# Experts' stage with exact high and low gather and scatter, a scatter in two parts and 2 MB weight units

## Chip, cores and metric

The kernel runs on one core of one Trainium2 chip. The metric is the device time of one execution in microseconds (us), the median of several runs; lower is better.

## What is computed

One step of a one-layer decoder, for 256 prompt tokens and 64 sample tokens (320 in all) that share the weights. A mixer (GLA attention and causal pooling) comes first, then a layer norm, then a mixture of experts, then a second layer norm. The change lies in the experts' stage. Cut to that:

```python
def _moe(x2, w_router, b_router, w_gu, b_gu, w_down, b_down):     # x2: 320 x 1024
    logits = x2 @ w_router + b_router
    top_v, top_i = lax.top_k(logits, 4)                  # 4 of 32 experts for each token
    gate_w = jax.nn.softmax(top_v, axis=-1)
    ...
    def expert_block(xblk, e):                           # the tokens that chose expert e
        hh = xblk @ w_gu[e] + b_gu[e]                    # 1024 x 2048 weights
        gate = jnp.minimum(hh[:, :1024], 7.0)
        up = jnp.clip(hh[:, 1024:], -7.0, 7.0)
        act = (up + 1.0) * (gate * jax.nn.sigmoid(1.702 * gate))
        return act @ w_down[e] + b_down[e]               # 1024 x 1024 weights
    ...
    y = y.at[token].add(gate_w * res)
x <- LayerNorm(alpha * h + moe(h))
```

All is float32. The weights of the 32 experts are 12 MB each (1 MB is 1024 x 1024 bytes here), 384 MB together, and each is read once.

## The kernel before

Every engine has its own program, and they meet at semaphores. The mixer ends with products of kind `out`; layer norm, router and ranks of each token tile run between the last of them (`turn_h`, `router`, `ranks`). The 320 tokens are tiles of 128, 128 and 64 rows (`TILES`), and each expert takes at most 64 tokens (`CAP`). More tokens for an expert would be worked off in an extra loop at the end.

The experts are worked off in 16 pairs, each pair by `pair_of_blocks` on TensorE (PE), ScalarE (ACT) and VectorE (DVE). For a pair of experts e and e+1, PE does in this order: `turn_up(e)` (8 transposes of the up product), `scatter` of the pair before, `expert_up` of e+1, `turn_slots`, `gather` for the next pair, `expert_down` of e, `turn_up(e+1)`, `expert_up` of e+2, `expert_down` of e+1. A gather is a product of the token rows `hrow` with a one-hot matrix of slots; its result is copied by ACT to `xgt`. A scatter is a product of the transposed one-hot matrix, which carries the gate weights, with the experts' output `res`; it gives six pieces of 128 (or 64) x 512, and DVE adds each to `y` (`add_pieces`). The pieces go through three PSUM banks, so the fourth has to wait for the first addition. PE runs a float32 product as two instructions, a product on a `float32r` view (`arena_r`, `ring_r`) as one.

The weights come as units of 1 MB, issued by the sync engine (SP) in the fixed order of `UNIT_SEQ`: 8 units for an up product, 4 for a down product. They lie in 16 slots (`SLOTS`). Twelve of the slots serve the mixer first and come free as its products end, so the first 16 units are loaded before the stage begins. After that SP issues unit n when PE has used unit n - 16:

```python
was_up, e, j = unit_at(n - SLOTS)
...
sp.wait_ge(up_used if was_up else down_used, count)
```

GpSimd (POOL) issues the small loads: `b_down` and the gains and biases of the second layer norm (`ln2`), both after the last router product. Between the first up product and the first pair, PE multiplies the gate weights with `b_down` (the line of `bdn_rows`), and DVE starts `y` with the six results. The parts named `first_gather`, `route` and `first_onehot` make the first gather, tile by tile, while the last tile is still in the layer norm.

## Time and profile before

| | |
|---|---|
| median of 3 runs | 1321.51 us (1321.49 to 1321.51) |
| the profiled execution | 1328.91 us, its span 1327.0 us |
| PE busy in the span | 1269.0 us (96%) |
| DVE, ACT busy | 437.7 us (33%), 230.6 us (17%) |
| first expert product starts, last ends | 347.74 us, 1302.65 us |
| last weight unit lands | 1289.4 us |
| moved by DMA | 454.19 MB, mean 342 GB/s over the span (417 GB/s in the stage) |
| granted TensorE clock | mean 0.983 |

The span runs from the first to the last instruction of the program; times inside it are counted from its start. MB and GB/s of the profile are in units of 10^6 and 10^9 bytes.

### The profile page before, as it was taken

The page shows a single profiled execution, that of the slowest core. Times are in us where ns is not written, and L with a number is a line of the kernel's source. Part 1 is how long each engine was busy: PE and PEld are TensorE (multiplying, and loading weights), DVE is VectorE, ACT ScalarE, POOL GpSimd, SP SyncE. Part 2 cuts the span into 40 slices and gives each one's busy share as a digit, 9 for nine tenths or more (in the row PEclk, how much of TensorE's full clock was granted, in tenths as well). Part 3 has the DMA queues.
Part 4 walks back from the last instruction along what each step waited for, and adds up shares of the span by engine and source line. Part 5 has one row for each costly group of instructions (what it writes and reads, how often), then busy time and mean ns, then how long its engine had stood idle before and what let it go on. Part 6 is the DMA issues. An engine that isn't in the chain of part 4 may idle for free.

```text
span 1327.0 us, 16958 instructions
## 1 busy us (share of the span) xinstructions
PE 1269.0 (96%) x6497; PEld 702.9 (53%) x6497; DVE 437.7 (33%) x871; ACT 230.6 (17%) x360; POOL 29.3 (2%) x43
## 2 busy tenths in 40 slices
PE   6999999999899999999999999999999999999993
PEld 6999999987543434343443434343443434343431
DVE  4665565654322241313132231313132231313135
ACT  4633334410101011011101011011101011011112
POOL 0000010200000000000000000000000000000002
PEclk9999999999789999999999999999999999999997
DMA  9524444673589999999999999999999999999981
GB/s 379 193 106 143 162 155 157 262 292 127 198 332 377 418 416 417 417 418 417 417 417 416 416 418 418 417 418 417 417 417 416 417 416 418 417 418 417 417 337 41
DMA packets 81366, 454.19 MB, mean 342 GB/s; under 512 B 7437, under 2 KB 7565, under 8 KB 44456
## 3 DMA queue, kind: packets, MB, share of 16 engines
q1 hardware_dynamic: 77264, 439.63, 82.0%
q0 software_dynamic: 4064, 14.03, 3.1%
q8 instruction: 27, 0.44, 0.1%
q14 instruction: 11, 0.09, 0.0%
HBM read 447.44 MB, written 6.31 MB: 342 GB/s over the span
## 4 chain that ended last, share of the span: by engine, by line
PE 92%; DVE 4%; issue 2%; DMA 1%; ACT 0%; DVEq 0%; SPq 0%; ACTq 0%
PE bank L919 33%; PE bank L942 17%; PE bank L649 13%; PE bank L898 10%; PE bank L963 4%; PE bank L717 3%; PE bank L692 2%; PE bank L928 1%; PE bank L931 1%; PE bank L774 1%; PE bank L857 1%; DVE arena L1610 1%; DVE arena L1597 1%; PE bank L906 1%; PE bank L741 1%
## 5 line engine op out<-in xcount | busy, mean ns | idle before, releaser
L919 PE MATMUL bank<-ring,arena 128*64 128x512 f32 x1536 | 349.6, 595 | 0.0
L919 PEld LDWEIGHTS bank<-ring,arena 128*64 128x64 f32 x1536 | 119.5, 137 | 205.8 <-issue 205.8
L649 PE MATMUL bank<-arena_r,ring_r 128*128 128x320 f32 x848 | 182.8, 316 | 0.0
L942 PE MATMUL bank<-ring,arena 128*64 128x512 f32 x768 | 169.3, 593 | 1.3 <-ACT arena L1212 1.3
L1588 DVE TENSOR_TENSOR arena<-bank,arena 128x512 f32<-128x512 f32 x64 | 41.2, 686 | 359.5 <-PE bank L931 359.5
L649 PEld LDWEIGHTS bank<-arena_r,ring_r 128*128 128x128 f32 x848 | 138.7, 188 | 1.9 <-issue 1.8
L1581 DVE COPY arena<-bank 128x512 f32<-128x512 f32 x32 | 22.1, 692 | 327.8 <-PE bank L919 327.6
L898 PE MATMUL bank<-arena 128*128 128x128 f32 x720 | 127.9, 308 | 0.0
L919 PE MATMUL bank<-arena 128*64 128x512 f32 x512 | 119.4, 593 | 1.4 <-ACT arena L1194 1.4
L963 PE MATMUL bank<-arena 128*128 128x512 f32 (+1 forms) x192 | 93.0, 613 | 21.7 <-DVE arena L1610 15.9
L898 PEld LDWEIGHTS bank<-arena 128*128 128x128 f32 x720 | 97.9, 188 | 28.1
L942 PEld LDWEIGHTS bank<-ring,arena 128*64 128x64 f32 x768 | 54.4, 137 | 107.7 <-issue 104.7
L1202 ACT ACTIVATE arena<-bank 128x512 f32<-128x512 f32 x32 | 19.1, 597 | 478.1 <-PE bank L919 478.1
L1274 DVE TENSOR_TENSOR ring_r<-ring,ring_r 128x1024 fp32r<-128x1024 f32 x56 | 67.7, 1222 | 57.4 <-ACT ring_r L1050 57.2
L649 PE MATMUL bank<-ring_r 128*128 128x320 f32 x280 | 85.9, 307 | 0.0
L919 PEld LDWEIGHTS bank<-arena 128*64 128x64 f32 x512 | 41.0, 136 | 70.9 <-issue 70.9
L1212 ACT ACTIVATE arena<-bank 64x512 f32<-64x512 f32 x64 | 37.8, 591 | 195.5 <-PE bank L942 195.1
L963 PEld LDWEIGHTS bank<-arena 128*128 128x128 f32 (+1 forms) x192 | 29.2, 171 | 75.8 <-DVE arena L1610 40.4
L1610 DVE TENSOR_TENSOR arena<-arena,bank 128x512 f32<-128x512 f32 (+1 forms) x96 | 62.9, 681 | 18.8 <-PE bank L963 18.4
L1050 ACT ACTIVATE ring_r<-ring 128x1024 fp32r<-128x1024 f32 x56 | 58.1, 1052 | 20.6 <-PE bank L649 19.3
L942 PE MATMUL bank<-arena 128*64 128x512 f32 x256 | 56.7, 595 | 0.0
L649 PEld LDWEIGHTS bank<-ring_r 128*128 128x128 f32 x280 | 52.7, 188 | 0.2
(213 smaller groups left out, 897.4 us busy)
## 6 DMA issues: line engine op xcount, KB each, us to landing
ring<-in_w_gu SPq DMA_DIRECT2D x192, 1024.0 KB, 14.9
ring<-in_w_down SPq DMA_DIRECT2D x96, 1024.0 KB, 17.8
arena<-in_w_gu SPq DMA_DIRECT2D x64, 1024.0 KB, 13.1
ring<-in_w_mix SPq DMA_DIRECT2D x32, 1024.0 KB, 5.1
arena<-in_w_down SPq DMA_DIRECT2D x32, 1024.0 KB, 16.5
arena<-in_state_gla POOLq DMA_DIRECT2D x4, 1024.0 KB, 10.3
out<-arena POOLq DMA_DIRECT2D x4, 1024.0 KB, 5.4
x_alone<-in_x_t SPq DMA_DIRECT2D x2, 640.0 KB, 4.6
```

The lines of the kernel that those rows point to most:

```text
L649: last = mm(o[:, 0:NT], w[a][:, c, f0:f0 + 128], rhs[b][:, c, :], start=c == 0 and a + b == 0, stop=c == chunks - 1 and a == 1)
L692: last = mm(o[:, 0:256], acts[c][:, t0:t0 + 128], w[:, c, :], start=c == 0, stop=c == KC - 1)
L717: last = mm(o[:, 0:256], xt[a][:, c, t0:t0 + 128], w[b][:, c, :], start=c == 0 and a + b == 0, stop=c == KC - 1 and a == 1)
L898: last = mm(ex[6 + c // 4][:, (c % 4) * 128:(c % 4 + 1) * 128], hrow[0:n, t, c * 128:(c + 1) * 128], onehot[0:n, t, :], start=t == 0, stop ...
L919: last = mm(ex[i][side * CAP:(side + 1) * CAP, :], xgt[:, j, half * CAP:(half + 1) * CAP], w[:, i * D + side * 512:i * D + (side + 1) * 51 ...
L942: last = mm(ex[4][side * CAP:(side + 1) * CAP, :], actt[:, 2 * j + c, :], w[:, c, side * 512:(side + 1) * 512], start=j == 0 and c == 0, s ...
L963: mm(ex[5 + i % 3][0:n, :], slot_t[:, t0:t0 + n], res[:, half * 512:(half + 1) * 512], start=True, stop=True).then_inc(pieces, 1)
L1050: A(half_of(hi, half), half_of(raw, half), ACT.Copy).then_inc(high_ready, 1)
L1212: last = A(res[half * CAP:(half + 1) * CAP, side * 512:(side + 1) * 512], ex[4][side * CAP:(side + 1) * CAP, :], ACT.Copy)
L1274: V.tensor_tensor(half_of(lo, half), half_of(raw, half), half_of(hi, half), ALU.subtract)\
L1588: V.tensor_tensor(dst.rearrange("p (h c) s -> p h c s", h=2), ex[2 + i][:, :].rearrange("p (c h s) -> p h c s", h=2, s=CAP), bias.broadcas ...
L1610: V.tensor_tensor(part, part, ex[5 + i % 3][0:n, :], ALU.add).then_inc(added, 1)
```

## The change

It has five parts.

1. **Gather.** `hrow` is split into a high part (a copy to `float32r`) and a low part (the remainder) by `split_h` on DVE. A gather multiplies both with the one-hot matrix: twice the products, on `float32r` views. It reports each half of the result, ACT copies each half by itself, and the up product waits for the second half only before its third unit. In the pair it stands behind the down product of e.
2. **Scatter.** The gate weight is no longer in the one-hot matrix. It is brought to the slots by six small products in `turn_slots` and applied when ACT copies the output (`keep_output`, high part) and when DVE makes the low part (`low_output`, new). The six pieces take two `float32r` products each, three pieces between the second and third unit of the up product and three behind its last (`between`). `turn_slots` stands between the two units of the down product.
3. **Down bias.** Three copies of gate weights and `b_down` are stacked on 96 partitions as high and low parts, and one `float32r` product gives each result.
4. **Units of 2 MB.** Eight slots of 2 MB; an up product has 4 units, a down product 2. The host lays the weights out so that a unit is one block with 16 KB on each partition.
5. **Places.** `y` takes the place of `hrow`, and the `ln2` values lie where a weight slot is, so POOL loads them once the first unit of the last expert has been used.

```diff
-SLOTS = MORE_AT + MORE
+SLOTS = (MORE_AT + MORE) // 2
+WIDE = 2 * UNIT
-UP_UNITS, DOWN_UNITS = KC, KC // 2
+UP_UNITS, DOWN_UNITS = KC // 2, KC // 4
...
+        LN2_FREE = (NE - 1) * UP_UNITS + 1
...
-                if is_up:
-                    src = w_gu[0, ds(e, 1), j * 128:(j + 1) * 128, :].rearrange("e p n -> p (e n)")
-                    sp.dma_start(dst, src).then_inc(filled[s], 16)
-                else:
-                    src = w_down[0, ds(e, 1), j * 256:(j + 1) * 256, :].rearrange("e (c p) n -> p (e c) n", p=128)
-                    sp.dma_start(dst.rearrange("p (c n) -> p c n", c=2), src).then_inc(filled[s], 16)
+                src = (w_gu if is_up else w_down)[ds(e, 1), j, :, :].rearrange("e p n -> p (e n)")
+                sp.dma_start(dst, src).then_inc(filled[s], 16)
...
-            pool.dma_start(bdn_rows, b_down[0, :, :]).then_inc(bdn_in, 16)
+            for i in range(3):
+                pool.dma_start(bdn_rows[i * NE:(i + 1) * NE, :], b_down[0, :, :]).then_inc(bdn_in, 16)
+            pool.wait_ge(up_used, LN2_FREE)
             pool.dma_start(ln2[0], ln2_g[0:1, :].broadcast_to([128, D])).then_inc(ln2_in, 16)
...
                 for c in range(KC):
                     for t, (t0, n) in enumerate(TILES):
-                        last = mm(ex[6 + c // 4][:, (c % 4) * 128:(c % 4 + 1) * 128], hrow[0:n, t, c * 128:(c + 1) * 128],
-                                  onehot[0:n, t, :], start=t == 0, stop=t == 2)
-                last.then_inc(gathered, 1)
+                        for a in range(2):
+                            last = mm(ex[6 + c // 4][:, (c % 4) * 128:(c % 4 + 1) * 128],
+                                      h_parts[a][t][0:n, c * 128:(c + 1) * 128], onehot[0:n, t, :],
+                                      start=t == 0 and a == 0, stop=t == 2 and a == 1)
+                    if c % 4 == 3:
+                        last.then_inc(gathered, 1)
...
                 for t, (t0, n) in enumerate(TILES):
-                    last = nc.tensor.transpose(ex[5][:, t0:t0 + n], onehot_w[0:n, t, :], ident[0:n, 0:n])
+                    mm(ex[5][:, t0:t0 + n], onehot[0:n, t, :], ident_r[0:n, 0:n], start=True, stop=True)
+                for t, (t0, n) in enumerate(TILES):
+                    for a in range(2):
+                        last = mm(ex[5][:, NT:NT + NE], onehot[0:n, t, :], gw_parts[a][0:n, t, :],
+                                  start=t == 0 and a == 0, stop=t == 2 and a == 1)
                 last.then_inc(slots_turned, 1)
...
+                    if gathers is not None and j % 2 == 0:
+                        pe.wait_ge(xgt_ready, 2 * gathers - 1 + j // 2)
                     pos, landing = where(j)
                     pe.wait_ge(*landing)
...
                     last.then_inc(up_used, 1)
+                    if j % 2 and between:
+                        between[j // 2]()
...
                     if i >= 3:
                         pe.wait_ge(added, pair * 6 + i - 2)
-                    mm(ex[5 + i % 3][0:n, :], slot_t[:, t0:t0 + n], res[:, half * 512:(half + 1) * 512],
-                       start=True, stop=True).then_inc(pieces, 1)
+                    for a in range(2):
+                        last = mm(ex[5 + i % 3][:, :], slot_t[:, t0:t0 + 128], res_parts[a][:, half * 512:(half + 1) * 512],
+                                  start=a == 0, stop=a == 1)
+                    last.then_inc(pieces, 1)
...
                 turn_up(e)
-                if not first:
-                    scatter(pair - 1, e)
-                expert_up(units(True, 2 * p + 1, m), 1)
-                turn_slots(pair + 1)
+                expert_up(units(True, 2 * p + 1, m), 1,
+                          between=() if first else [lambda: scatter(pair - 1, e, 0), lambda: scatter(pair - 1, e, 1)])
...
-                else:
+                if not first:
+                    pe.wait_ge(added, pair * 6 - 2)
+                expert_down(e, units(False, 2 * p, m), between=turn_slots)
+                if not last:
                     if not first:
                         pe.wait_ge(added, pair * 6)
                     gather(pair + 2)
-                expert_down(e, units(False, 2 * p, m))
...
+            def low_output(idx, half):
+
+                dve.wait_ge(res_high, idx + 1)
+                p0 = half * CAP
+                for side in range(2):
+                    f0 = side * 512
+                    last = V.scalar_tensor_tensor(res_parts[1][p0:p0 + CAP, f0:f0 + 512], ex[4][side * CAP:(side + 1) * CAP, :],
+                                                  slot_w[p0:p0 + CAP, 0:1], res_parts[0][p0:p0 + CAP, f0:f0 + 512],
+                                                  ALU.mult, ALU.subtract)
+                last.then_inc(res_ready, 1)
```

How PE's instructions move shows best where no loop registers stand between them. In the first pair, behind the transposes of expert 0, PE's rows before are the up product (L919) of expert 1, the slots' transposes (L906), the gather (L898), the down product (L942), the transposes for expert 1 (L928, L931), the next up product and the second down product:

```order
L919 MATMUL bank<-ring,arena 64x512 x32
L906 MATMUL bank<-arena 128x128 x2
L906 MATMUL bank<-arena 128x64
L898 MATMUL bank<-arena 128x128 x24
L942 MATMUL bank<-arena 64x512 x16
L928 MATMUL bank<-arena 128x128 x4
L931 MATMUL bank<-arena 128x128 x4
L919 MATMUL bank<-ring,arena 64x512 x32
L942 MATMUL bank<-ring,arena 64x512 x16
```

In the changed program the same place reads as follows (L948 is now the up product, L974 the down product, L928 and L931 the turning of slots and of gate weights, L919 the gather, L960 and L963 the transposes):

```order
L948 MATMUL bank<-ring,arena 64x512 x32
L974 MATMUL bank<-arena 64x512 x8
L928 MATMUL bank<-arena_r 128x128 x2
L928 MATMUL bank<-arena_r 128x64
L931 MATMUL bank<-arena_r 128x32 x6
L974 MATMUL bank<-arena 64x512 x8
L919 MATMUL bank<-arena_r 128x128 x48
L960 MATMUL bank<-arena 128x128 x4
L963 MATMUL bank<-arena 128x128 x4
L948 MATMUL bank<-ring,arena 64x512 x32
L974 MATMUL bank<-ring,arena 64x512 x16
```

The gather has twice the products and now stands behind the down product; the turning of the slots stands inside it.

The scatter is seen in the last pair. Before, PE's rows there are the transposes, the scatter (L963), and then the whole up product:

```order
L928 MATMUL bank<-arena 128x128 x4
L931 MATMUL bank<-arena 128x128 x4
L963 MATMUL bank<-arena 128x512 x4
L963 MATMUL bank<-arena 64x512 x2
L919 MATMUL bank<-arena 64x512 x16
L919 MATMUL bank<-ring,arena 64x512 x16
```

In the changed program L998 is the scatter:

```order
L960 MATMUL bank<-arena 128x128 x4
L963 MATMUL bank<-arena 128x128 x4
L948 MATMUL bank<-arena 64x512 x16
L998 MATMUL bank<-arena_r 128x512 x6
L948 MATMUL bank<-ring,arena 64x512 x16
L998 MATMUL bank<-arena_r 128x512 x6
```

It is cut in two, and an up product's half stands ahead of each part. On DVE, also in the last pair, the additions of the pieces stood before in one row of six ahead of the copy of the up product:

```order
L1610 TENSOR_TENSOR arena<-arena,bank 128x512 x4
L1610 TENSOR_TENSOR arena<-arena,bank 64x512 x2
L1575 TENSOR_SCALAR arena<-arena 128x64 x2
L1575 TENSOR_SCALAR arena<-arena 64x64
L1575 TENSOR_SCALAR arena<-arena 128x64 x2
L1575 TENSOR_SCALAR arena<-arena 64x64
L1581 COPY arena<-bank 128x512
```

Now three of them stand ahead of that copy (L1633) and three behind it:

```order
L1662 TENSOR_TENSOR arena<-arena,bank 128x512 x3
L1633 COPY arena<-bank 128x512
L1662 TENSOR_TENSOR arena<-arena,bank 128x512
L1662 TENSOR_TENSOR arena<-arena,bank 64x512 x2
```

The one-hot matrices with weights (L1575) are gone from DVE.

## Rows read from the trace of the kernel before

**Rows 1.** Page: GB/s moved by DMA in 40 equal slices of the span

```profile
GB/s 379 193 106 143 162 155 157 262 292 127 198 332 377 418 416 417 417 418 417 417 417 416 416 418 418 417 418 417 417 417 416 417 416 418 417 418 417 417 337 41
```

**Rows 2.** Waits of PE, 377 to 1286 us: who for whom, total, times, longest

```profile
PE bank L963 <- DVE arena L1610: 15.9, 15, 1.1
PE bank L963 <- ACT arena L1212: 4.6, 15, 0.4
```

**Rows 3.** Timeline of PE, one pair and more: start, us, instruction, idle before

```profile
605.97 0.66 PE L928 MATMUL bank<-arena 128*128 128x128 f32 x4
...
613.72 14.27 PE L919 MATMUL bank<-ring,arena 128*64 128x512 f32 x63
627.92 0.64 PE L906 MATMUL bank<-arena 128*128 128x128 f32 x3
628.49 8.52 PE L898 MATMUL bank<-arena 128*128 128x128 f32 x48
...
643.96 0.66 PE L928 MATMUL bank<-arena 128*128 128x128 f32 x4
...
644.99 13.95 PE L919 MATMUL bank<-ring,arena 128*64 128x512 f32 x64
...
687.69 0.64 PE L906 MATMUL bank<-arena 128*128 128x128 f32 x3
```

**Rows 4.** DMA, two windows of 60 us (600:660, 1160:1220): issues, KB, median us to landing

```profile
ring<-in_w_gu SPq DMA_DIRECT2D x12, 1024.0 KB, 13.3
...
ring<-in_w_gu SPq DMA_DIRECT2D x16, 1024.0 KB, 17.8
```

**Rows 5.** Four single issues (1236.6, 1249.8, 1251.5, 1270.9 us): landing min/median/max

```profile
DMA to landing us min/median/max: 14.8/14.8/14.8
...
DMA to landing us min/median/max: 19.1/19.1/19.1
...
DMA to landing us min/median/max: 19.9/19.9/19.9
...
DMA to landing us min/median/max: 18.5/18.5/18.5
```

**Rows 6.** Windows: us, PE, PEld, DVE, ACT, POOL busy, PEclk, DMA share, GB/s

```profile
349.70:1289.40 939.70, 917.32 (x4231) 385.96 (x4229) 226.13 (x506) 98.52 (x171) 0.00 (x0) 0.99 1.00 411
```

**Rows 7.** Timeline of SP, its first issue in the stage, and that issue's landing

```profile
349.71 5.52 SPq L515 DMA_DIRECT2D arena<-in_w_down  x4
...
DMA to landing us min/median/max: 4.9/4.9/4.9
```

**Rows 8.** Line L717: durations in ns (min/median/max), first and last start

```profile
L717 PE MATMUL bank<-ring_r,arena_r x192: 277/280/283, 46.6 to 80.2; 128*128 128x256 f32 x192
```

**Rows 9.** Timeline around the stage's start

```profile
322.91 9.85 PE L857 MATMUL bank<-arena 64*128 64x128 f32 x32 [0.56 <-issue]
343.06 3.31 PE L857 MATMUL bank<-arena 128*128 128x128 f32 x16 [0.34 <-DVE arena L1521]
347.74 7.09 PE L919 MATMUL bank<-arena 128*64 128x512 f32 x32 [1.38 <-ACT arena L1194]
361.63 0.55 PE L1001 MATMUL bank<-arena 128*32 128x128 f32 x3
363.12 7.72 PE L1009 MATMUL bank<-arena 32*128 32x512 f32 x12 [0.94 <-DVEq L1675]
371.61 1.11 PE L928 MATMUL bank<-arena 128*128 128x128 f32 x4 [0.77 <-DVE arena L1681]
```

**Rows 10.** Windows of lost clock, columns as in rows 6

```profile
325.30:345.70 20.40, 17.55 (x70) 14.41 (x69) 6.17 (x32) 2.99 (x6) 1.59 (x3) 0.50 0.25 83
366.30:376.40 10.10, 9.33 (x22) 3.30 (x22) 5.12 (x10) 0.63 (x1) 0.00 (x0) 0.50 0.58 240
```

**Rows 11.** Chain that ended last, the stage's end: start, us, what

```profile
1295.54 7.11 PE bank L942 x32
```

**Rows 12.** Page, costliest groups: x count, busy us, mean ns, idle before

```profile
L1581 DVE COPY arena<-bank 128x512 f32<-128x512 f32 x32 | 22.1, 692 | 327.8 <-PE bank L919 327.6
```

More of the change, by code:

```diff
@@ L156 @@
 ARENA = MISC + 64
-H = 0
-Y = 3072
-XGT = 6144
-OHW = 7168
-ACTT = 7552
-G1 = 8064
-OH = 8704
-U1 = 9088
-SG = 9600
-HG = 10112
-HU = 10624
-RES = 11136
-RK = 12352
-GW = 12832
-MSK = 12928
-LG = 13024
-MX = 13120
-RT = 13152
-LISTS = 13536
-GWT = 14120
-BDR = 14440
-LN2 = BDR + D
-ST = LN2 + 2 * D
+Y = 0
+RK = 3072
+GW = 3552
+MSK = 3648
+LG = 3744
+RES = 3840
+MX = 4864
+RT = 4872
+LISTS = 5256
+XGT = 5816
+ACTT = 6840
+SLOT_T = 7352
+WS = 7672
+G1 = 7680
+U1 = 8192
+LOW1 = 8704
+SG = 9728
+HIGH_H = VR
+LOW2 = KLT
+OH = 14336
+IDR = 14720
+HG = 14848
+HU = 15360
+BDR = 15872
+GWT = 16896
+GWR = 17216
+LOW0 = 17408
 MORE_SLOTS = 18432
+LN2 = MORE_SLOTS
 def build(nc, x_p, x_s, state_gla, state_pool, w_gk2, w_grp,
@@ L311, in build @@
         low = ar[0:1, LISTS + 4 * NID + RANKS:LISTS + 4 * NID + 2 * RANKS]
-        filled = [sem(f"slot{i}_filled") for i in range(SLOTS)]
+        filled = [sem(f"slot{i}_filled") for i in range(MORE_AT + MORE)]
         bank_full = [sem(f"bank{i}_full") for i in range(8)]
@@ L850, in released, with first_gather @@
                 pe.wait_ge(bank_free[n], LAST_USE[n])
-            def first_gather(tiles, first):
-                for c in range(KC):
+            def first_gather(tiles, half, first):
+                for c in range(4 * half, 4 * half + 4):
                     for t in tiles:
                         n = TILES[t][1]
-                        last = mm(ex[6 + c // 4][:, (c % 4) * 128:(c % 4 + 1) * 128], hrow[0:n, t, c * 128:(c + 1) * 128],
-                                  onehot[0:n, t, :], start=first and t == tiles[0] and c % 4 == 0, stop=not first,
-                                  skip_group_check=True)
+                        for a in range(2):
+                            last = mm(ex[6 + half][:, (c % 4) * 128:(c % 4 + 1) * 128], h_parts[a][t][0:n, c * 128:(c + 1) * 128],
+                                      onehot[0:n, t, :], start=first and t == tiles[0] and a == 0 and c % 4 == 0,
+                                      stop=not first and a == 1, skip_group_check=True)
                 return last
@@ L880, in _ @@
             pe.wait_ge(onehot_early, 1)
-            first_gather(ORDER[:2], True)
+            pe.wait_ge(parts_ready, 2)
+            for half in range(2):
+                first_gather(ORDER[:2], half, True)
             turn_h(1, 5)
@@ L981, in pair_of_blocks @@
                     gather(pair + 2)
[L982 to L983 removed]
                     turn_up(e + 1)
[L985 to L987 removed]
+                    expert_up(units(True, 2 * p + 2, m), 0, gathers=pair + 2)
                 pe.wait_ge(res_ready, e + 1)
@@ L992, in _ @@
             pe.wait_ge(onehot_ready, 1)
-            first_gather(ORDER[2:], False).then_inc(gathered, 1)
+            pe.wait_ge(parts_ready, 3)
+            for half in range(2):
+                first_gather(ORDER[2:], half, False).then_inc(gathered, 1)
             released(0)
             released(1)
-            pe.wait_ge(xgt_ready, 1)
-            expert_up(units(True, 0), 0)
+            expert_up(units(True, 0), 0, gathers=1)
             pe.wait_ge(soft4_done, 1)
@@ L1602, in gated, with add_pieces @@
                 V.tensor_tensor(actt[:, :, :], u1[:, :, :], sg[:, :, :], ALU.mult).then_inc(act_ready, 1)
-            def add_pieces(pair):
-                for i in range(6):
+            def add_pieces(pair, part):
+                for i in range(3 * part, 3 * part + 3):
                     t, half = i // 2, i % 2
```

239 lines of the change are left out of this document (144 added, 95 removed).

## The prediction

> **What bounds the kernel now.** I read the page's slices first. From slice 14 on DMA moves 416 to 418 GB/s without a break [rows 1], so the stage looks bound by the weight loads. The waits say otherwise: between 377 and 1286 us PE waits 20.5 us in all, only inside the scatter (L963), for an addition or for ACT, and never for a weight [rows 2]. The timeline of PE gives its period: the slots' transposes (L906) stand at 627.92 and at 687.69 us, so a pair takes PE 59.77 us [rows 3]. A pair reads 24 units, 25.17 million bytes, which at 417 GB/s is 60.35 us [rows 1]. So the loads are the slower of the two by 0.6 us a pair. PE does not feel it, because 16 MB lay in the slots when the stage began. The stock shrinks: the median time from issue to landing grows from 13.3 us (window from 600 us) to 17.8 us (from 1160 us) [rows 4], while one issued onto idle queues lands after 4.9 us [rows 7]. PE has its last product at 1302.65 us [rows 11], 13.3 us behind the last landing at 1270.9 + 18.5 = 1289.4 us [rows 5]. The kernel is bound by PE, with the loads close behind: time taken from PE comes back only until the loads bind. So I need two end times, that of PE and that of the loads.
>
> **PE's pair.** Each term is a difference of starts in [rows 3] or a count times a row.
> - Scatter: from the first transposes of a pair (605.97) to its up product (613.72) are 7.75 us, where the same transposes elsewhere take 644.99 - 643.96 = 1.03. The scatter costs 6.7 us, its waits included. It becomes 12 float32r products of 512 columns. The row of such products is L717 with 256 columns: 288 of them (3 tiles x 4 units x 24) between 46.6 and 80.3 us, 117 ns each [rows 8]. Twice the columns give 0.22 us; the upper bound is the present float32 instruction's 0.43 us for 512 columns (an up product's 64 run two side by side, 32 x 0.43 = 13.95 us [rows 3]). I take 0.22, the nearer kind: 2.6 us (at most 5.2).
> - Gather: 8.5 us for 48 instructions (L898) now. Then again 48, of 128 columns each, as float32r. If they cost no more than the 256-column ones they take 48 x 0.117 = 5.6 us; if the weight loads of 64 rows cost as now, up to 8.5. I take 6.0, near the row of their kind.
> - Turning the slots: 627.92 to 628.49, 0.57 us now; then 9 float32r products at 0.117 or more, 1.2 us.
> - New wait: the down product waits for the fourth addition of a pair. DVE copies the up product (0.69 us [rows 12]) between the third and fourth addition, so the fourth ends near 1.5 us after the up product, PE's second scatter part near 1.3. I take 0.3 us. Behind that wait are the down product and SP's release of its slots. The two waits of rows 2 go: half an up product, 6.9 us, lies between the parts.
> - DVE and ACT: `low_output` adds 2 x 0.69 us a block, the two rows of one-hot matrices with weights go. DVE sits idle 328 us before L1581 alone [rows 12], which hides it; without that cover it would cost 2.8 us a pair.
>
> Sum: 59.77 - 6.7 + 2.6 - 8.5 + 6.0 - 0.57 + 1.2 + 0.3 = 54.1 us a pair, 5.7 less (bounds 53.3 and 59.2).
>
> **The stage's start.** The first gather (tiles 2 and 0) takes 9.85 us, the second 3.31, and then up to 347.74 ACT copies both halves [rows 9]. With the first as 32 instructions of half the columns' time I take 2.3 us off (from 0 to 6). The second can hand over its first half after half its length, so its copy and the other half overlap: 1.7 us off. The stage then starts at 347.7 - 4.0 = 343.7 us (338 to 348). The new splits of `h` on DVE, two passes for each tile, about 2.5 us a tile by row 12's rate, lie where DVE waits for PE's products or for the router. The bias: from 361.63 to the first transposes at 371.61 are 10 us [rows 9], with 12 instructions in 7.72 us. Six float32r products make DVE's six additions the bound, 6 x 0.72 = 4.3 us, plus a second DVE pass: 3.5 us less, so the gap is 6.5.
>
> **PE's end.** 1302.65 - 4.0 - 3.5 - 14 x 5.7 - 5 (what the first and the last pair save) = 1210 us.
>
> **The loads' end.** Here 2 MB units matter. Landings: 8 KB rows (`w_gu`), 7 units from 1236.6 + 14.8 to 1249.8 + 19.1, 2.50 us each; 4 KB rows (`w_down`), 7 units from 1251.5 + 19.9 to 1289.4, 2.56 us each [rows 5]. Each of 16 DMA engines moves 8 rows of 8 KB in 2.50 (0.3125 us a row) or 16 of 4 KB in 2.56 (0.160). Another 4 KB costs 0.1525, so a row has 0.0075 of its own. A 16 KB row is 0.3125 + 2 x 0.1525 = 0.6175: 8 of them make a 2 MB unit in 4.94 us. Were the row's own cost nothing, 4.88; if longer rows gain nothing, 5.00; at today's mean (60.35 / 12) 5.03. I take 4.92, between the line and its lower end, as the first figure hangs on landings read to 0.1 us.
>
> By the Trainium skill, "DMA: Bandwidth & Descriptors", section "Where 436 GB/s comes from", the ceiling is 435 GB/s at SBUF's ports, by which a 2 MB unit would take at least 4.82 us, an estimate from that page; by it the loads would end 18 us sooner than in my sum. The same page of the skill puts an HBM limit of about 358 GB/s for a core beside it; this trace disagrees, with 417 GB/s over 900 us.
>
> Eight units, 16 MB as now, are in place before the stage. The ninth is issued when PE has used the first: its 16 instructions take 3.43 us (64 in 13.7). To its first byte go 4.9 - 2.5 = 2.4 us. So the loads start at 343.7 + 5.8 = 349.5. Up(0) frees four units, 19.7 us of loads, done at 369; the next slot comes free after up(0), the bias, the transposes and 3.4 us: 343.7 + 13.7 + 6.5 + 1.1 + 3.4 = 368.4, with 2.4 us latency 370.8, more at half clock, which the old trace had from 366.3 to 376.4 [rows 10]. I take 4 us of idle queues. Before, this idle and more of its kind was 939.7 us [rows 6] less 368 units x 2.515 = 14 us. Then 184 units: 184 x 4.92 = 905.3. The `ln2` loads, 1 MB in 4 KB rows, now fall into the loaded stretch: 2.6. The loads end at 349.5 + 4 + 905.3 + 2.6 = 1261.4 us, 51 us behind what PE could do. **So PE will wait for weights, and the loads set the end.** The moved `b_down` copies fall where the queues are idle (198 GB/s in slice 11 [rows 1]) and cost nothing; in the loaded stretch they would cost 1 us.
>
> **The end.** The last unit is worked off in 3.43 + 0.6 = 4.0 us. From the last product to the end are 1327.0 - 1302.65 = 24.35 us; `low_output` adds 1.4, six additions that wait no more for float32 products take off about 1.2: 24.6. Span: 1261.4 + 4.0 + 24.6 = 1290.0, 37.0 less than 1327.0. The profiled execution took 1328.91 us, 7.4 more than the median; I take the difference off the median: 1321.5 - 37.0 = **1284.5 us**.
>
> **Rivals.**
> 1. The loads bind but gain nothing from long rows (5.03 instead of 4.92): 184 x 0.11 = 20 us more, 1305 us. For it: a mean rate constant for 900 us looks like a ceiling. Against it: 8 KB rows land faster than 4 KB rows.
> 2. The clock. The granted clock was 0.50, its level of 1.2 GHz, from 325.3 to 345.7, after the gather's short products of 64 rows, and from 366.3 to 376.4, in the bias products of 32 rows [rows 9, 10]; each time PE had instructions nearly all the time. The new gather streams half as long per weight load as the old, and PE then waits for weights. If each gather costs the clock for the shorter of those stretches, 10.1 us, PE loses 5 us a pair and ends at 1210 + 14 x 5.05 = 1281 us, behind the loads: 1281 + 24.6 - 1327 = -21.4, 1300 us.
> 3. The same for the longer stretch, 20.4 us, 10.2 lost a pair: PE's end 1210 + 143 = 1353, span 1377.5, **1372 us, slower**. It decides from 6.6 us lost a pair (14 x 6.6 = 92, PE's old end). Against both: the old gather, 8.5 us with 64-row products too, kept full clock in all 14 pairs (clock 0.99 over the stage [rows 6]), and up products follow at once. The Trainium skill, "TensorE: Matmul & The Clock Gate", section "HAM oscillation", tells of a kernel that lost the clock again and again as it waited for weights; the trace of before has no such wait to show.
> 4. PE gains but the loads were the true bound already, so nothing moves: 1321 us. Rows 2 and 11 speak against it.
>
> **Numbers.** Forecast case 0.64, rival 1 0.16, rival 2 0.11, rival 3 0.06, rival 4 0.03. The forecast's bounds: 4.88 takes off 7 us and a start at 338 another 6, so 1270; rival 1 reaches 1305 at the top, which also holds rival 2. The range 1270 to 1306 leaves out rivals 3 and 4 and some of the tails. Less than 0.2% (2.6 us) cannot be told from no change: faster 0.91, same 0.03, slower 0.06.
>
> **What would show it.** A pair takes about 54 us while the stock of 16 MB lasts (PE gains one 2 MB unit a pair), then 12 x 4.92 = 59 us, with PE waiting for weight loads about 5 us a pair; about 426 GB/s; the last landing near 1261 us and PE's last product 4 us behind it; gather near 6 us, scatter parts 1.3 us each without idle. I am wrong if a pair stays near 60 us with no wait for a load (PE slower than I think), if GB/s stays at 417 (rival 1), or if the clock row shows less than full in the stage (rivals 2, 3).

## The result and the profile after

The changed kernel takes **1340.0 us** (median of 4 executions, 1338.3 to 1341.0), and the ratio to the kernel before is 1.0112, with an interval of 1.0083 to 1.0141: slower by 1.1%, where 1284.5 us was forecast. (Executions of the kernel before take 1321.0 to 1331.8 us, most of them near 1321.5 or 1329, with a mean clock from 0.990 down to 0.980; every ratio is to executions of it on the same chip.) In the profiled executions the span went from 1327.0 to 1337.8 us.

The page after, its slices (PEclk is the granted TensorE clock in tenths; the last row answers to [rows 1]):

```profile
span 1337.8 us, 16365 instructions
...
PE   6999999999899999999999999999999999999993
...
PEclk9999999998788998989898898989898998989897
...
GB/s 378 196 109 131 172 142 158 281 267 126 212 370 329 427 420 404 430 398 429 422 429 402 428 401 410 417 421 430 402 427 400 428 422 417 414 399 429 402 269 41
```

DMA now swings between 400 and 430 GB/s, so the loads are no longer back to back. PE is busy without a break, by the profile, which models the ends of its products, and the clock row dips all through the stage. Of the waits of PE over the whole span (who for whom, total, times, longest, answering to [rows 2]) none is for a weight. These are the three longest; the two for DVE, which makes the low part of the output in L1670, are single waits of the last pair:

```profile
PE bank L681 <- ACT ring_r L1088: 10.2, 1, 10.2
PE bank L974 <- DVE arena_r L1670: 3.1, 1, 3.1
PE bank L998 <- DVE arena_r L1670: 3.1, 1, 3.1
```

So PE sets the end. Its timeline over one pair (start, us, instruction) answers to [rows 3]. L919 is the gather, L960 and L963 are transposes, L948 up products, L974 down products, L998 the scatter's two parts, L928 and L931 `turn_slots`:

```profile
637.05 9.38 PE L919 MATMUL bank<-arena_r 128*128 128x128 f32 x48
646.35 1.11 PE L960 MATMUL bank<-arena 128*128 128x128 f32 x4
647.26 1.06 PE L963 MATMUL bank<-arena 128*128 128x128 f32 x4
648.25 14.45 PE L948 MATMUL bank<-ring,arena 128*64 128x512 f32 x64
662.53 7.03 PE L974 MATMUL bank<-ring,arena 128*64 128x512 f32 x32
669.50 0.66 PE L960 MATMUL bank<-arena 128*128 128x128 f32 x4
...
670.52 7.09 PE L948 MATMUL bank<-arena 128*64 128x512 f32 x32
677.54 1.66 PE L998 MATMUL bank<-arena_r 128*128 128x512 f32 x6
679.13 7.09 PE L948 MATMUL bank<-ring,arena 128*64 128x512 f32 x32
686.15 1.67 PE L998 MATMUL bank<-arena_r 128*128 128x512 f32 x6
687.75 3.65 PE L974 MATMUL bank<-ring,arena 128*64 128x512 f32 x16
691.33 0.66 PE L928 MATMUL bank<-arena_r 128*128 128x128 f32 x3
691.92 0.94 PE L931 MATMUL bank<-arena_r 128*128 128x32 f32 x6
692.79 3.65 PE L974 MATMUL bank<-ring,arena 128*64 128x512 f32 x16
696.38 10.30 PE L919 MATMUL bank<-arena_r 128*128 128x128 f32 x48
```

Three things are to be seen. The scatter comes near the forecast: two parts of 1.60 us (677.54 to 679.13, and 686.15 to 687.75) where 1.3 each were forecast, without a wait. The gather does not: 9.38 and 10.30 us where 6.0 was forecast and 8.52 stood before. And the same four transposes take 1.11 us behind the gather and 0.66 us later on: the clock is at half there. Two windows put on such stretches, and one behind them (columns as in [rows 6]):

```profile
581.00:591.20 10.20, 10.20 (x36) 6.70 (x38) 3.27 (x6) 1.23 (x2) 0.00 (x0) 0.50 1.01 430
642.50:649.30 6.80, 6.80 (x26) 5.26 (x28) 0.83 (x2) 0.60 (x1) 0.00 (x0) 0.50 1.00 426
651.00:663.00 12.00, 12.00 (x60) 3.91 (x58) 1.09 (x3) 0.25 (x1) 0.00 (x0) 1.00 1.00 411
```

A clock of 0.50 is the 1.2 GHz level, 1.00 is 2.4 GHz. PE was busy for all of the 10.2 and 6.8 us in which it had lost half of its clock. In each of the 15 gathers of the stage's pairs the clock falls, 3.2 to 5.7 us after the gather's start: 4 times for 6.8 us, 10 times for 10.2 us, and the first for 13.7 us. Fourteen pairs go by from the first of these gathers (393.47) to the last (1241.37), 60.56 us each, against 59.77 before.

### The profile page after: what moved, and what is told of

Its sections match the earlier page's. It is cut to its first block, busy times and chain, and to the rows that moved or that the text cites. A ratio compares the mean times of both kernels' runs of the same rounds, so it can differ in the third digit from the quotient of the medians.

```text
span 1337.8 us, 16365 instructions
## 1 busy us (share of the span) xinstructions
PE 1295.3 (97%) x6587; PEld 746.3 (56%) x6587; DVE 467.8 (35%) x812; ACT 245.3 (18%) x394; POOL 30.4 (2%) x45
## 4 chain that ended last, share of the span: by engine, by line
PE 96%; DVE 2%; DMA 1%; ACT 0%; issue 0%; DVEq 0%; SPq 0%; ACTq 0%
PE bank L948 35%; PE bank L974 17%; PE bank L666 13%; PE bank L919 11%; PE bank L998 4%; PE bank L734 3%; PE bank L709 2%; PE bank L960 2%; PE bank L963 2%; PE bank L791 1%; PE bank L931 1%; PE bank L875 1%; PE bank L928 1%; PE bank L758 1%; DMA ring<-in_w_mix 1%; PE bank L721 1%
## 5 line engine op out<-in xcount | busy, mean ns | idle before, releaser
L948 PE MATMUL bank<-ring,arena 128*64 128x512 f32 x1536 | 360.1, 626 | 0.0
L948 PEld LDWEIGHTS bank<-ring,arena 128*64 128x64 f32 x1536 | 111.2, 145 | 227.3 <-issue 227.3
L974 PE MATMUL bank<-ring,arena 128*64 128x512 f32 x768 | 171.0, 594 | 3.1 <-DVE arena_r L1670 3.1
L919 PE MATMUL bank<-arena_r 128*128 128x128 f32 x720 | 146.7, 343 | 0.0
L919 PEld LDWEIGHTS bank<-arena_r 128*128 128x128 f32 x720 | 124.2, 234 | 31.8 <-issue 12.2
L1633 DVE COPY arena<-bank 128x512 f32<-128x512 f32 x32 | 22.1, 692 | 279.9 <-PE bank L948 279.4
L948 PE MATMUL bank<-arena 128*64 128x512 f32 x512 | 114.9, 602 | 0.0
L1670 DVE SCALAR_TENSOR_TENSOR arena_r<-bank,arena,arena_r 64x512 fp32r<-64x512 f32 x64 | 48.0, 750 | 187.0 <-ACT arena_r L1256 186.6
L974 PEld LDWEIGHTS bank<-ring,arena 128*64 128x64 f32 x768 | 52.8, 137 | 107.7 <-issue 100.9
L1320 DVE TENSOR_TENSOR ring_r<-ring,ring_r 128x1024 fp32r<-128x1024 f32 x56 | 67.7, 1223 | 56.8 <-ACT ring_r L1088 56.6
L948 PEld LDWEIGHTS bank<-arena 128*64 128x64 f32 x512 | 36.0, 139 | 71.3 <-issue 71.1
L1256 ACT ACTIVATE arena_r<-bank,arena 64x512 fp32r<-64x512 f32 x64 | 43.7, 683 | 147.0 <-PE bank L974 146.6
L974 PE MATMUL bank<-arena 128*64 128x512 f32 x256 | 58.4, 598 | 0.0
L998 PE MATMUL bank<-arena_r 128*128 128x512 f32 x192 | 53.3, 413 | 3.1 <-DVE arena_r L1670 3.1
L998 PEld LDWEIGHTS bank<-arena_r 128*128 128x128 f32 x192 | 33.4, 188 | 34.8 <-issue 24.7
```

Of the source, the lines that this page charges most:

```text
L919: last = mm(ex[6 + c // 4][:, (c % 4) * 128:(c % 4 + 1) * 128], h_parts[a][t][0:n, c * 128:(c + 1) * 128], onehot[0:n, t, :], start=t == 0 ...
L948: last = mm(ex[i][side * CAP:(side + 1) * CAP, :], xgt[:, 2 * j + c, half * CAP:(half + 1) * CAP], w[:, c, i * D + side * 512:i * D + (sid ...
L974: last = mm(ex[4][side * CAP:(side + 1) * CAP, :], actt[:, 4 * j + c, :], w[:, c, side * 512:(side + 1) * 512], start=j == 0 and c == 0, s ...
L998: last = mm(ex[5 + i % 3][:, :], slot_t[:, t0:t0 + 128], res_parts[a][:, half * 512:(half + 1) * 512], start=a == 0, stop=a == 1)
L1256: last = A(res_parts[0][p0:p0 + CAP, side * 512:(side + 1) * 512], ex[4][side * CAP:(side + 1) * CAP, :], ACT.Copy, scale=slot_w[p0:p0 + C ...
L1320: V.tensor_tensor(half_of(lo, half), half_of(raw, half), half_of(hi, half), ALU.subtract)\
```

## The experiments

Two theories stood at the start. **A**: the clock. The new gather streams little for each load of weights, the clock falls to half under it, and PE loses some 4 us a pair; with the clock kept, PE is faster than the loads and the time is near the forecast. **B**: not the products but the gather's new place costs the time. Unless it says otherwise, an edit is to the changed kernel.

| run | gather at work, us | pair, us (first / loads bound) | mean clock | median, us | ratio to before, interval |
|---|---|---|---|---|---|
| changed kernel | 9.1 to 10.9 | 60.6 / - | 0.929 | 1340.0 | 1.011 (1.008 to 1.014) |
| e1_float32 | 8.5 | 57.1 / 58.8 | 0.981 | 1299.4 | 0.982 (0.979 to 0.986) |
| e1_filler | 9.6 | 58.2 / - | 0.981 | 1305.5 | 0.991 (0.986 to 0.995) |
| e1_pad | 5.4 | 54.0 / 58.8 | 0.979 | 1300.1 | 0.983 (0.980 to 0.986) |
| e1_quarters | 4 x 1.9 | 56.8 / 58.8 | 0.982 | 1295.5 | 0.980 (0.977 to 0.984) |
| e2_both | 4 x 1.5 | 54.9 / 58.8 | 0.978 | 1298.5 | 0.977 (0.974 to 0.981) |
| e2_rows8 | 4 x 1.5 | 54.9 / 59.8 | 0.983 | 1310.5 | 0.987 (0.984 to 0.990) |
| e2_first | 4 x 1.5 | 54.9 / 58.8 | 0.983 | 1292.7 | 0.973 (0.969 to 0.977) |
| e2_units | 8.5 | 59.8 / - | 0.990 | 1326.8 | 0.999 (0.997 to 1.001) |
| e3_ln2 | 4 x 1.5 | 54.9 / 58.8 | 0.984 | 1288.1 | 0.970 (0.968 to 0.972) |
| e3_grouped | 5.9 to 8.1 | 54.6 / 58.8 | 0.966 | 1297.8 | 0.978 (0.975 to 0.982) |
| e4_thin | 15.4 to 17.2 | 67.0 / - | 0.900 | 1436.6 | 1.082 (1.078 to 1.087) |

The gather is timed from its start to that of the next instruction. A pair is the difference of two gathers' starts; the first value holds while the stock of 16 MB lasts. Gather, pair and mean clock are those of the profiled execution, the median is that of all executions.

### The cause: four ways to keep the clock

**e1_float32** leaves the low part out of the gather and runs the high part as float32, two instructions a product, in the same place:

```diff
-                        for a in range(2):
-                            last = mm(..., h_parts[a][t][0:n, c * 128:(c + 1) * 128], onehot[0:n, t, :],
-                                      start=t == 0 and a == 0, stop=t == 2 and a == 1)
+                        last = mm(..., h_parts[0][t][0:n, c * 128:(c + 1) * 128].bitcast(f32),
+                                  onehot[0:n, t, :].bitcast(f32), start=t == 0, stop=t == 2)
```

> The gather of every pair as float32 products of the high part alone (the low part of h is left out of these gathers), at the place it has in the changed kernel. Theory A (the clock falls in the gather because its float32r products stream too thinly between weight loads): the gather takes 8.5 us as in the kernel before and the clock stays at full speed in the stage; a pair is 57.2 us of PE (56.3 of the changed kernel at full clock, less 7.6, plus 8.5), less than the 58.8 us of the loads, so the loads bind: about 1295 us. Theory B (it is the place: gather and transposes behind each other after the down product): the clock falls in every pair as before, a pair is near 62 us, about 1365 us.

**e1_filler** adds work: one product of 512 columns, whose result nobody reads, behind each of the gather's eight chunks.

```diff
                     if c % 4 == 3:
                         last.then_inc(gathered, 1)
+                    mm(ex[2][:, :], h_parts[0][0][:, 0:128], h_parts[0][0][:, 0:512], start=True, stop=True)
```

> One float32r product of 512 columns, whose result nothing reads, after each of the eight chunks of the gather: 8 x 0.22 = 1.7 us more work for PE in a pair. Theory A: the clock stays at full speed, a pair is 58.1 us, just under the loads: about 1297 us, 43 faster with more work. If the clock is not what the changed kernel lost its time by: 15 x 1.7 = 26 us slower, about 1366 us.

**e1_pad** makes the third tile's 64 rows 128, with zeros in the rows of `h_parts` that hold no token:

```diff
-                                      h_parts[a][t][0:n, c * 128:(c + 1) * 128], onehot[0:n, t, :],
+                                      h_parts[a][t][:, c * 128:(c + 1) * 128], onehot[:, t, :],
```

> The last token tile padded from 64 to 128 rows in the gather (zero rows), so all 48 products are 128 x 128 and PE never changes between tiles of 64 and 128 rows. Same count of products. Theory A: 48 x 0.112 = 5.4 us for the gather, streaming in 48% of the time instead of 33%; the clock stays full, a pair is 54.1 us, the loads bind, about 1293 us, with PE waiting for weights 4 to 5 us a pair. Theory B: the clock still falls in each pair and the time is nearer to 1300 to 1310 us.

**e1_quarters** keeps the products and spreads them: a quarter of the gather inside the down product ahead of it, one behind it, and two inside the first unit of the next up product.

```diff
-                    gather(pair + 2)
+                    gather_quarter(pair + 2, 1)
                     turn_up(e + 1)
-                    expert_up(units(True, 2 * p + 2, m), 0, gathers=pair + 2)
+                    expert_up(units(True, 2 * p + 2, m), 0, gathers=pair + 2, quarters=True)
```

> The same gather products in four quarters, two around the second half of the down product and two between the first chunks of the next up product. No instruction is added or taken away. Theories A and B: no thin stretch is longer than 3 us, the clock stays full, a pair is 56.3 us and the loads bind: about 1295 us. If the clock is not the cause: no change against 1340 us.

All four have medians of 1296 to 1306 us. Theory B falls with the first: same place, a gather of 8.5 us, and 41 us less. The filler is the strictest of them. It gives PE 2.0 us more to do in every pair (9.6 instead of 7.6 us at full clock) and takes away no product, no wait and no change of height, and the median is 34 us lower. It does not keep the clock every time, though: six of its ten executions took 1304.8 to 1305.7 us with a mean clock of 0.981, the other four 1323.0 to 1325.6 us with 0.966 or 0.965. Where those four lost it isn't shown, as none of them was profiled; all ten stay below the changed kernel. In one window, 660 to 1200 us, the changed kernel, then the filler (columns of [rows 6]):

```profile
660.00:1200.00 540.00, 540.00 (x2473) 247.01 (x2471) 140.23 (x243) 64.38 (x117) 0.00 (x0) 0.92 0.99 416
```

```profile
660.00:1200.00 540.00, 540.00 (x2639) 244.63 (x2637) 147.98 (x257) 65.68 (x119) 0.00 (x0) 1.00 1.01 428
```

PE is busy for all 540 us in both; at clock 1.00 it gets through 2639 products instead of 2473, some 74 of them the filler's. The same window of e1_float32, e1_pad and e1_quarters:

```profile
660.00:1200.00 540.00, 535.32 (x2584) 231.67 (x2580) 145.40 (x253) 65.75 (x121) 0.00 (x0) 1.00 1.01 428
...
660.00:1200.00 540.00, 505.53 (x2568) 220.18 (x2562) 142.53 (x248) 67.16 (x123) 0.00 (x0) 1.00 1.01 428
...
660.00:1200.00 540.00, 532.99 (x2591) 230.50 (x2590) 144.67 (x252) 65.38 (x123) 0.00 (x0) 1.00 1.01 428
```

The expected times were 4 us (float32), 7 us (padding) and 8.5 us (filler) too low; that of e1_quarters was right to 1 us. In e1_filler PE is still the bound, at 58.2 us a pair and without a wait for a weight, where I had counted on the loads. In e1_pad the last weight lands at 1262.2 us as reckoned, but the clock falls to half in the last products: the last down product takes 8.78 us, as in e1_filler, and 7.09 in e1_quarters.

**e3_grouped** adds nothing and takes nothing away. It puts the gather's products in another order, so that full and half height alternate less:

```diff
-                for c in range(KC):
-                    for t, (t0, n) in enumerate(TILES):
+                for half in range(2):
+                    for t, (t0, n) in enumerate(TILES):
+                        for c in range(4 * half, 4 * half + 4):
```

> The changed kernel with the gather's products in another order: for each half of the columns first the 16 products of tile 0 and 1, then the 8 of tile 2 (64 rows) in one row, so that the height of the products changes 4 times instead of 16. Theory S (the change of height costs, 50 to 95 ns each): the gather takes 5.6 to 6.2 us at full clock instead of 7.6. Theory H (a product of 64 rows is itself slow): it stays at 7.6. For the clock no cure is expected for sure: the stream gets denser than in the changed kernel and stays thinner than in the padded one. If the clock still falls in each pair: 14 x 1.5 to 2.5 us less than 1340, about 1310 to 1320 us; if it is kept, about 1297 us.

Its timeline, three gathers:

```profile
612.66 6.00 PE L920 MATMUL bank<-arena_r 128*128 128x128 f32 x48
618.60 0.66 PE L961 MATMUL bank<-arena 128*128 128x128 f32 x4
...
668.12 6.00 PE L920 MATMUL bank<-arena_r 128*128 128x128 f32 x48
674.06 0.91 PE L961 MATMUL bank<-arena 128*128 128x128 f32 x4
...
726.94 6.43 PE L920 MATMUL bank<-arena_r 128*128 128x128 f32 x48
733.30 1.11 PE L961 MATMUL bank<-arena 128*128 128x128 f32 x4
```

Theory S of its expectation holds: 6.00 us at full clock, the very term of the prediction. The same 48 products need 7.6 us in the changed kernel's order (four quarters of 1.91 us by their starts in e1_quarters, at full clock). So this order is a cure in part only: in or right behind 6 of the 15 gathers the clock is lost, for 3.4 to 10.2 us (mean over 660 to 1200 us: 0.97). I had put the median at 1310 to 1320 us for "falls in each pair" and 1297 for "kept"; it is 1297.8, since the loads bind and PE has 4 us of room in each pair.

**e4_thin** is the test from the other side. It starts from e1_pad, where all products have 128 rows, and cuts each into two of 64 columns:

```diff
-                    for t, (t0, n) in enumerate(TILES):
+                    for s, t in ((0, 0), (0, 1), (0, 2), (1, 0), (1, 1), (1, 2)):
...
-                                      h_parts[a][t][:, c * 128:(c + 1) * 128], onehot[:, t, :],
+                                      h_parts[a][t][:, c * 128:(c + 1) * 128], onehot[:, t, s * 64:(s + 1) * 64],
```

> The padded kernel, with each product of the gather cut into two of 64 columns: all 96 products have 128 rows, none changes height, and PE is never idle between them; they stream the same columns in all, and load the weights twice as often. Theory A (thin streaming behind full weight loads loses the clock, at any height): if a product of 64 columns takes as long as one of 128 (about 110 ns) the gather takes 10.5 us, the clock falls in every pair, and a pair takes 54.0 + 5 + 4 to 5 = about 63 to 64 us, median about 1380 to 1400 us. Theory H (the change between 64 and 128 rows loses the clock): the clock stays full, a pair takes about 59 us, median about 1300 to 1310 us. If a product of 64 columns takes half as long, the stream is as dense as before the cut and both expect the padded kernel's time.

```profile
654.23 3.65 PE L974 MATMUL bank<-arena 128*64 128x512 f32 x16
...
659.28 3.65 PE L974 MATMUL bank<-arena 128*64 128x512 f32 x16
662.86 16.27 PE L919 MATMUL bank<-arena_r 128*128 128x64 f32 x96
678.95 1.11 PE L960 MATMUL bank<-arena 128*128 128x128 f32 x4
```

Two windows in this gather, before and behind the fall of the clock (columns of [rows 6]):

```profile
662.86:667.60 4.74, 4.74 (x45) 4.74 (x43) 1.49 (x2) 1.37 (x2) 0.00 (x0) 1.00 1.02 432
...
667.80:678.90 11.10, 11.10 (x54) 11.10 (x53) 0.00 (x0) 0.60 (x1) 0.00 (x0) 0.50 1.01 430
```

The clock falls in every gather, for 13.7 or 17.1 us, and the kernel takes 1436.6 us. Theory H, that the change of height loses the clock, falls: there is no such change here. A falls short in size only (1380 to 1400 expected), as the clock was lost for most of the gather itself, 16.1 us instead of 10.5. PE was never idle in it. So a run of products that stream few columns for each load of weights loses the clock by itself.

The run is also twice as long as that of e1_pad, but length alone does not explain the fall: it comes 3.7 to 5.7 us after the gather's start, in 13 of the 15 gathers within 5.36 us, and the padded gather of e1_pad, 5.41 us long, keeps the clock in all 15. Length counts beside it, as e1_quarters shows: the changed kernel's own products keep the clock in pieces of 1.9 us.

### What binds once the clock is kept

**e2_both** joins e1_quarters and e1_pad; **e2_rows8** is the same with each unit fetched in two transfers:

```diff
-                sp.dma_start(dst, src).then_inc(filled[s], 16)
+                for i in range(2):
+                    sp.dma_start(dst[:, i * UNIT:(i + 1) * UNIT], src[:, i * UNIT:(i + 1) * UNIT]).then_inc(filled[s], 16)
```

> The changed kernel with the gather in quarters and its third tile padded to 128 rows, both at once. Theory A (with the clock kept, the weight loads set the end): PE alone would need 54.0 us a pair (measured in the padded version while the stock lasted) against 58.8 us of loads, so the second cure adds nothing to the first: the last weight lands near 1262 us as in the padded version, PE keeps its clock to the end, median near 1292 us. Rival C (PE sets the end): the pair loses another 2.8 us against the quarters alone, 14 x 2.8 = 39 us less than 1295.5, about 1257 us.

> The same kernel as e2_both with each 2 MB unit fetched by two transfers of 1 MB, whose rows are 8 KB again instead of 16 KB; slots, waits and products stay. Theory A: a unit takes 2 x 2.50 = 5.00 us instead of 4.90, so 184 x 0.10 = 18 us more than e2_both, about 1311 us, and 60.0 us a pair while the loads bind. Rival 1 of the prediction (long rows gain nothing): the same time as e2_both, within 2 us.

The second cure on top of the first gives nothing that can be told (ratio 0.977 and 0.980, intervals overlap), although PE's pair is 1.9 us shorter while the stock lasts. Its waits between 1000 and 1200 us say why:

```profile
PE bank L949 <- DMA ring<-in_w_gu: 6.8, 8, 1.2
PE bank L978 <- DMA ring<-in_w_down: 2.2, 3, 0.7
PE bank L949 <- DMA arena<-in_w_gu: 1.4, 2, 1.2
```

PE waits for weights, and the window from 660 to 1200 us shows it idle for 28 us with DMA at 428 GB/s (540.00 - 512.27):

```profile
660.00:1200.00 540.00, 512.27 (x2559) 217.60 (x2556) 141.97 (x248) 65.44 (x122) 0.00 (x0) 1.00 1.01 428
```

Rival C falls. The median of e2_both is 6.5 us above the 1292 expected, though the last weight lands at 1264.4 us, 0.1 behind that of e1_quarters: the clock falls three times near the end, so that the last down product takes 8.78 and the scatter behind it 5.49 us, against 7.09 and 3.44. Rival 1 of the prediction falls too: with rows of 8 KB the same window moves 421 GB/s, a pair takes 59.8 us instead of 58.8, the last weight lands at 1278.8 us, and the median is 12 us higher. (Row length and number of transfers change together here; which of the two costs the time is not shown.) I had expected 18 us, from 2.50 us a MB against 2.45; the landings in e2_rows8 are 2.49 us apart.

**e2_units** is the kernel before with the 2 MB units alone (slots, layout, waits of the diff, nothing else).

> The kernel before with nothing of the change but the 2 MB units: 8 slots of 2 MB, rows of 16 KB, waits for a unit twice as large. Theory A (the kernel before is bound by PE): the loads gain 1.3 us a pair that PE does not ask for, so the median stays at 1321.7 us within 2 us. Rival 4 of the prediction (the loads were the bound already): 184 x 0.12 = 22 us less, about 1300 us.

The ratio is 0.999 (0.997 to 1.001), and a pair takes the 59.8 us of before: the faster loads are of no use as long as PE binds. (Its 1326.8 us stand against 1328.8 us, the median of the kernel before on that chip.) Rival 4 falls.

**e2_first** is e2_both with the third tile padded in `first_gather` too, and **e3_ln2** is e2_first with POOL waiting for the last weight unit before it loads `ln2`:

```diff
             pool.wait_ge(up_used, LN2_FREE)
+            pool.wait_ge(*landed(NE * EXP_UNITS - 1))
```

> The same kernel as e2_both with the third tile padded in the first gather too, so that its first part (8.4 us) has no products of 64 rows. Theory A: that part falls to about 4 to 5.5 us, the clock stays at its full level ahead of the stage or falls for a shorter time, the stage starts 2 to 4 us earlier, and as the loads are released by the first up product, the end moves by as much: about 1289 us. Rival D (the router's chain on DVE, not PE's gather, sets the stage's start): no change against e2_both.

> The same kernel as e2_first, with the two transfers of the last norm's gain and bias released by the landing of the last weight unit instead of by the use of the first up unit of the last block. Theory A (the queue of weight loads sets the end): the three late units that land 5.4, 6.2 and 5.7 us apart come 4.9 us apart again, the last weight lands 2.5 us earlier, PE's longest wait for a weight (2.5 us) goes; if with it the clock stays full in the last products, another 1 to 3 us: 3 to 6 us less than e2_first, about 1288 us. Rival E: the transfers, now last, land after DVE has asked for them, and the end stays where it is or moves back.

The stage's start in e2_both:

```profile
323.06 8.14 PE L875 MATMUL bank<-arena_r 64*128 64x128 f32 x32 [0.56 <-issue]
...
341.44 3.68 PE L875 MATMUL bank<-arena_r 128*128 128x128 f32 x16 [0.34 <-DVE arena_r L1578]
345.04 9.30 PE L949 MATMUL bank<-arena 128*64 128x512 f32 x32
```

And in e2_first:

```profile
322.35 3.76 PE L875 MATMUL bank<-arena_r 128*128 128x128 f32 x32 [0.56 <-issue]
...
333.92 3.67 PE L875 MATMUL bank<-arena_r 128*128 128x128 f32 x16 [0.34 <-DVE arena_r L1578]
337.52 8.80 PE L949 MATMUL bank<-arena 128*64 128x512 f32 x32
```

The first part's 32 instructions take 3.76 instead of 8.14 us, although they work on a third more rows, zeros. In e2_both the clock is at half from 325.7 us on, for 23.9 us, in e2_first from 330.8 on, for 10.2. The stage starts 7.5 us earlier (2 to 4 expected), the last weight lands 8.5 us earlier (1255.9), and the span is 8.6 us shorter (5.8 us in the medians, where the intervals of the ratios overlap). Rival D falls. One of the four executions of e2_first had a mean clock of 0.936 instead of 0.983 and yet took 1295.2 us, 2.5 above the median, which fits that a lost clock costs little while the loads bind. In e3_ln2 the last weights come 4.9 us apart again and the last lands at 1253.3 us, 2.6 us earlier, and PE's longest wait for a weight goes from 2.5 to 1.3 us; the span is 3.4 us shorter, 4.6 us in the medians. So the end did not stay where it was, as rival E has it, by the two traces; the intervals of the ratios overlap here too. The clock in the last products did not come back, though: the last down product takes 8.78 us and the scatter 5.49 in both. This is the lowest median, 1288.1 us, 3.0% below the kernel before (2.8 to 3.2%).

## Why the prediction was wrong

The step that failed is the one on **the clock**, rivals 2 and 3, to which it gave 0.17 together. The reason given against them was that "the old gather, 8.5 us with 64-row products too, kept full clock in all 14 pairs". But the old gather was float32, with two instructions for each product; e1_float32 shows that this kind keeps the clock in the new place too. What the runs show instead is a loss at every one of the 15 new gathers, 4.3 us a pair, which e1_filler, e1_quarters, e3_grouped and e4_thin lay to a long run of thinly streaming products. The prediction had seen that the new gather "streams half as long per weight load as the old" and weighed it too lightly. The nearest row was the first gather of the kernel before, 9.85 us long, 2.4 us into which the clock had fallen, at 325.3 [rows 9, 10]. The clock was lost for 6.8 or 10.2 us a time, near rival 2's 10.1, and rival 2 gave 1300 us, not a loss. What made it rival 3's outcome, a slower kernel, is that further terms were too small, the gather's above all, in which the changes of height stood at nothing:

- **PE's pair**, forecast 54.1 us. Scatter 3.2 instead of 2.6; `turn_slots` 1.46 (691.33 to 692.79) instead of 1.2; the new wait 0 instead of 0.3. That gives 54.1 + 0.6 + 0.3 - 0.3 = 54.7, and e3_grouped, whose gather takes the forecast 6.0, has a pair of 54.6. The gather in the changed order takes 1.6 us more (56.2), and the lost clock the remaining 4.3: 60.56. PE thus loses 6.5 us a pair against the forecast; the prediction had put the point of no gain at 6.6.
- **PE's end**, forecast 1210 us, is 1306.37 + 7.09 = 1313.5. Of the 103 us, 14 x 6.45 = 90 are the pairs' and 1.3 the stage's start (345.0 instead of 343.7); the other 12 lie in the first and the last pair and the up product ahead of them, where the clock was at half too (from 325.0 to 348.9 and from 366.0 to 372.8 us). They are not split further.
- **The stage's start and the bias.** The first gather took 8.4 instead of the 7.6 us implied (9.85 - 2.3). Both stood under a clock at half (from 325.0 us here), so 9.85 us was no price at full clock; e2_units below has that price. The six stacked products and the rest up to the first transposes took 6.7 us (360.8 to 367.6), 6.5 forecast.
- **The loads.** 4.92 us a unit was forecast, 4.90 measured, in every version of 16 KB rows that they bind; 5.00 for 8 KB rows, 4.98 measured. The end of the loads, forecast at 1261.4 us, is 1264.2 in e1_quarters, which makes the same products as the changed kernel at full clock; PE's last product is 4.4 us behind it (4.0 forecast), 24.4 us before the end (24.6), and the span 1293.1 (1290.0). The side of the sum that hangs on "PE will wait for weights" is near the mark once PE keeps its clock, in part because errors offset: 184 units at 4.90 take 3.7 us less than at 4.92, the stage starts 1.3 later, and some 5 us more lie elsewhere and are not split further. (The 417 GB/s "over 900 us" of the prediction hold for some 830 us, 25 slices; over the 940 us of [rows 6] it is 411.) In the changed kernel itself the loads have room, and the last one lands at 1293.6 us because PE frees the slots late.
- **DVE**, costed at nothing, cost nothing in the pairs: PE waits for it in none, and only at the stage's end for `low_output`, twice 3.1 us.
- **The difference of 7.4 us** between the profiled execution and the median was taken off the forecast. The changed kernel has no such second value (1338.3 to 1341.0), so its profiled execution, 1339.7, stands at its median. The profiled execution of e2_units, 1321.65 us, shows where the 7 us lie: its products are those of the kernel before, but its clock is at half from 334.4 us on for 6.8 us, not from 325.2 on for 20.5. The first gather, 9.85 us in [rows 9], takes 6.71 us, and the stage starts at 342.1 instead of 347.7 us:

```profile
322.40 6.71 PE L853 MATMUL bank<-arena 64*128 64x128 f32 x32 [0.56 <-issue]
```

## What to carry to other kernels

A product's price is not its duration in a dense row alone: ask how many columns each load of weights is followed by, and count a long run of short products as a risk for the clock, in the run and behind it, even when the engine never idles. Before halving the streaming time of a run of products, look in the trace for a run of the new kind and read the clock in it and behind it; when it falls, spread the run or pad it (the clock held in all 15 gathers), or order it by height (it held in 9 of 15 gathers). Read the mean clock of several executions too, not of the profiled one alone. And a second bound that is close (here 58.8 us of loads against 59.8 of PE) caps the gain, so that a cure is worth making only up to it.

## What the runs showed of the hardware

- The clock fell to half with PE busy for 100% of the time by the profile, in all 15 gathers of the changed kernel. Waits for weights of up to 1.3 us, again and again, left it at 1.00 from 660 to 1200 us (28 of 540 us in e2_both). Longer single waits went either way: at one of 2.5 us for a weight near the end it fell for 3.4 us in e1_float32, e1_pad, e2_both and e2_first and stayed full in e1_quarters, as it did at one of 2.9 us in e2_rows8. The Trainium skill, "TensorE: Matmul & The Clock Gate", section "HAM oscillation", lays a lost clock to waits for transfers, and section "Why this matters for your kernels" advises against long idle gaps of PE between its bursts. The falls at the waits near the end, in four of the six versions named, point the same way; the loss in the changed kernel is one that no gap explains.
- Going from 128 to 64 rows and back between float32r products of 128 columns costs: 7.6 us for 48 products with 16 changes a gather, 6.0 with 4, so (7.6 - 6.0) / 12 = 0.13 us a change. With the short tile padded, a fifth more rows to work on, the gather took 5.4 us.
- A float32r product of 64 columns takes no less time than one of 128. At full clock the starts in the gather are 112 ns apart in e4_thin (64 columns) and 111 ns in e1_pad (128 columns, all of 128 rows), by the median; at half clock they are 213 ns apart in e4_thin.
- A 2 MB unit in 16 KB rows lands every 4.90 us, 428 GB/s; in two transfers of 8 KB rows every 4.98 us, 421 GB/s.
